# Order of the first mixer: value tiles beside the first modulation tiles, gates behind them, then queries and keys

## The reference

```python
def modulate(h, shift, scale):
    return h * (1.0 + scale[:, None, :]) + shift[:, None, :]

sh1, sc1, g1, sh2, sc2, g2 = jnp.split(jnp.einsum('bd,de->be', jax.nn.silu(c), ada_w) + ada_b, 6, axis=-1)
h = modulate(rmsnorm(x, norm_mix_g), sh1, sc1)
y = mlstm_mixer(h, ...)          # below
x = x + g1[:, None, :] * y

def mlstm_mixer(h, w_in, conv_w, b_if, hnorm_g, w_out):
    proj = jnp.einsum('bsd,de->bse', h, w_in)
    qk, v, o, gates = jnp.split(proj, ...)       # 1024, 1024, 1024 and 16 columns
    q, k = jnp.split(jax.nn.silu(causal_conv(qk, conv_w)), 2, axis=-1)
    ...                                          # per head: decays from the gates, scores q k, times v, over a denominator
    hh = rmsnorm(hh, hnorm_g) * jax.nn.sigmoid(o)
    return jnp.einsum('bse,ed->bsd', hh, w_out)
```

## Time and profile before

| | |
|---|---|
| median of 3 runs | 2536.34 us (2536.04 to 2536.48) |
| profiled execution, its span | 2535.0 us |
| PE busy in the span | 2494.9 us (98%) |
| DVE, ACT, POOL busy | 2040.5, 1492.4, 345.5 us |
| moved by DMA | 509 MB, 201 GB/s on average |

### The profile page before, as it was taken

How to read it: one execution, slowest core, us unless ns; L and a number is a source line. 1 busy time by engine, 2 the same in 40 slices (tenths; PEclk the granted TensorE clock), 3 DMA queues, 4 the chain that set the end, 5 groups by cost and what they waited for, 6 DMA issues and landing times.

```text
span 2535.0 us, 44017 instructions
## 1 busy us (share of the span) xinstructions
PE 2494.9 (98%) x14932; PEld 2170.5 (86%) x14932; DVE 2040.5 (80%) x3770; ACT 1492.4 (59%) x2489; POOL 345.5 (14%) x212
## 2 busy tenths in 40 slices
PE   7999999999999999999999999999999999999998
PEld 6789988888888888889988888888888888899887
DVE  7789979899888877679888998666667886688766
ACT  4455576666666656555677666665564555463553
POOL 4017600000000003527500000000000001000000
PEclk8999999999999999999999999999999999999999
DMA  7854576776888885435666776566555355553654
GB/s 270 284 167 165 195 238 191 201 208 204 302 292 288 284 258 162 142 122 170 210 217 193 206 199 209 183 200 202 194 191 190 127 188 184 193 177 107 199 183 141
DMA packets 142991, 509.07 MB, mean 201 GB/s; under 512 B 19200, under 2 KB 19256, under 8 KB 142560
## 3 DMA queue, kind: packets, MB, share of 16 engines
q1 hardware_dynamic: 135600, 481.90, 57.3%
q0 software_dynamic: 7216, 24.85, 5.1%
HBM read 488.84 MB, written 1.07 MB: 193 GB/s over the span
## 4 chain that ended last, share of the span: by engine, by line
PE 87%; DVE 5%; DMA 4%; ACT 2%; issue 1%; POOL 1%; SPq 0%; DVEq 0%; ACTq 0%
PE ps L243 51%; PE ps L249 19%; PE ps L250 9%; DMA weight_ring<-in_stream 4%; PE ps L1528 2%; ACT weight_split L269 1%; DVE weight_split L278 1%; POOL weight_split L278 1%; PE ps L2735 1%; PE ps L1492 1%; DVE arena L745 0%; DVE hT_split L503 0%; PE ps L457 0%; DVE stat L628 0%; DVE x L625 0%
## 5 line engine op out<-in xcount | busy, mean ns | idle before, releaser
L269 ACT ACTIVATE weight_split<-weight_ring 128x1024 fp32r<-128x1024 f32 x800 | 848.8, 1062 | 224.5 <-DMA weight_ring<-in_stream 132.9
L243 PE MATMUL ps<-weight_split,hidden_split 128*128 128x512 f32 x3948 | 911.8, 390 | 0.4 <-DVE hidden_split L1821 0.3
L278 DVE TENSOR_TENSOR weight_split<-weight_ring,weight_split 128x1024 fp32r<-128x1024 f32 x653 | 791.4, 1221 | 135.2 <-ACT weight_split L269 132.0
L243 PEld LDWEIGHTS ps<-weight_split,hidden_split 128*128 128x128 f32 x3948 | 736.0, 188 | 157.1 <-issue 1.0
L249 PE MATMUL ps<-hT_split,weight_split 128*128 128x512 f32 x2000 | 721.9, 402 | 0.5 <-DVE hT_split L503 0.4
L250 PE MATMUL ps<-hT_split,weight_split 128*128 128x256 f32 x2000 | 559.5, 280 | 0.0
L243 PE MATMUL ps<-hT_split,weight_split 128*128 128x256 f32 x3672 | 462.8, 285 | 3.0 <-DVE hT_split L503 0.8
L243 PEld LDWEIGHTS ps<-hT_split,weight_split 128*128 128x128 f32 x3672 | 447.3, 192 | 10.3 <-issue 5.9
L249 PEld LDWEIGHTS ps<-hT_split,weight_split 128*128 128x128 f32 x2000 | 375.7, 188 | 84.5 <-DVE hT_split L503 1.1
L250 PEld LDWEIGHTS ps<-hT_split,weight_split 128*128 128x128 f32 x2000 | 377.8, 189 | 2.6
L278 POOL TENSOR_TENSOR weight_split<-weight_ring,weight_split 128x1024 fp32r<-128x1024 f32 x115 | 279.1, 2433 | 115.5 <-ACT weight_split L269 85.2
(11 more groups left out here) (381 smaller groups left out, 2078.3 us busy)
## 6 DMA issues: line engine op xcount, KB each, us to landing
weight_ring<-in_stream SPq DMA_DIRECT2D x912, 512.0 KB, 4.2
weight_split<-weight_ring POOLq DMA_DIRECT2D x32, 512.0 KB, 5.3
arena<-gate_rows SPq DMA_DIRECT2D x3, 512.0 KB, 4.8
x<-in_x SPq DMA_DIRECT2D x1, 1024.0 KB, 5.1
arena<-mlstm_m_rows POOLq DMA_DIRECT2D x1, 1024.0 KB, 6.5
arena<-in_ln_mix_g POOLq DMA_DIRECT2D x2, 512.0 KB, 5.8
arena<-in_ln_mix_b POOLq DMA_DIRECT2D x2, 512.0 KB, 7.8
arena<-in_ln_ffn_g POOLq DMA_DIRECT2D x2, 512.0 KB, 4.7
```

The source lines that it names most:

```text
L243: mm = pe.matmul(out_, stationary(s_part), moving(m_part), start=start and n == 0, stop=stop and n == 2, skip_group_check=True)
L269: act.activation(wsplit[:, n % SPLITS, HIGH, :], ring[:, slot(POS[n]), :], ACT.Copy).then_inc(high_ready, 1)
L278: eng.tensor_tensor(w[:, REST, :], ring[:, slot(POS[n]), :], w[:, HIGH, :].bitcast(fp32), ALU.subtract).then_inc(split_ready, 1)
```

## The change

- The 16 first modulation tiles are reordered and all are dots now: scale chunk c, shift chunk c, for c = 0 to 7. After each pair DVE adds the bias and finishes the gain of that one chunk (`first_mods_dve`), so each chunk of the normed input can be made at once.
- Eight value tiles are the first tiles of TensorE. They and the modulation tiles 16 to 21 come through six further slots in `arena` (`side`), loaded by SP between the ring's loads. TensorE multiplies value tile c when chunk c is there, and the gates of chunk c-2 behind it. The 80 idle transposes are gone.
- Queries and keys follow, then the heads. The second half's modulation tiles (16 to 38) are all used in the head stage, three per head where there were two, and 39 in the output stage.
- The rests of value tiles 0 to 5, of all queries and keys and of all eight output-gate tiles are made by POOL; DVE makes those of value tiles 6 and 7 and of the output stage.
- silu of c is computed on a row that the DMA has spread over the partitions (512 KB written), in place of a spreading by TensorE.

The stream keeps its tiles and their number; their order and the part that comes by `side` are changed.

```diff
+V_TILES, SIDE, SIDE_ADA = 8, 6, range(16, 22)
-SEGMENTS = [("ada", "a", 16), ("mlstm", "s", 8), ("mlstm_v", "sa", 8), ("mlstm_o", "saa", 7), ("mlstm_o_end", "sa", 1),
-            ("mlstm_out", "s", 4), ("mlstm_out_ada", "sa", 1), ("mlstm_out_end", "s", 3),
+SEGMENTS = [("ada", "a", 16), ("mlstm", "s", 8), ("mlstm_o", "s", 4), ("mlstm_o_ada", "aaas", 4), ("mlstm_o_end", "a", 3),
+            ("mlstm_out", "s", 2), ("mlstm_out_ada", "a", 2), ("mlstm_out_mid", "s", 3), ("mlstm_last_ada", "a", 1), ("mlstm_out_end", "s", 3),
...
+        def first_dot_dve(a, products):
+            c, row = a // 2, 1 - a % 2
...
+            dve.tensor_tensor_reduce(products, ada_loaded(a), silu_row[:], 1.0, 0.0, ALU.mult, ALU.add, dots[:, row, c:c + 1]).then_inc(ada_used, 1)
...
         def mlstm_pool():
...
-            rests_pool(ML_T + 1, 3)
+            rests_pool(ML_V, 6)
+            rests_pool(ML_T, 4)
 
             pool.wait_ge(ml_gate_dve, M_READY)
             pool.dma_start(ml_rows.rearrange("(h t) -> h t", t=T), ml_M).then_inc(ml_M_moved, 16)
-            for n in range(ML_T + 4, ML_T + 6):
-                rest(pool, n)
+            rest(pool, ML_T + 4)
             pool.wait_ge(ml_M_moved, M_OUT)
             pool.dma_start(ml_Mb.rearrange("p h t -> p (h t)"), ml_rows.partition_broadcast(128)).then_inc(ml_M_moved, 16)
-            for n in range(ML_T + 6, ML_T + 10):
+            for n in range(ML_T + 5, ML_H + 8):
                 rest(pool, n)
...
+            def beside_v(c):
+                if c == 2:
+                    pe.wait_ge(ml_par, 16 * 7)
+                    pe.wait_ge(gate_w_ready, 1)
+                if c >= 2:
+                    gates(c - 2)
+            lin_rows(ML_V, 0, 0, between=beside_v)
+            gates(6)
+            gates(7).then_inc(ml_gates, 1)
...
         def mlstm_act():
...
+            high(ML_V)
+            modulated(0)
+            for c in range(1, 8):
+                modulated(c)
+                high(ML_V + c)
             highs_act(ML_T, 3)
...
         def mlstm_dve():
...
+            for c in range(8):
+                first_dot_dve(2 * c, ml_acc[:, 1])
...
+                first_dot_dve(2 * c + 1, ml_acc[:, 1])
+                first_mods_dve(c)
...
+                if c:
+                    chunk_split_dve(c - 1)
+            chunk_split_dve(7)
+            splits_until(dve, ML_V + 6)
+            rest(dve, ML_V + 6)
+            rest(dve, ML_V + 7)
...
-                    for a in (26 + 2 * h, 27 + 2 * h):
+                    for a in range(19 + 3 * h, 22 + 3 * h):
                         ada_dve(a, ml_acc[:, 1])
...
                 if h == 6:
-                    gated(6)
-                    ada_dve(38, ml_acc[:, 1])
+                    for a in (37, 38):
+                        ada_dve(a, ml_acc[:, 1])
+                    splits_until(dve, ML_O)
                     rest(dve, ML_O)
+                    rest(dve, ML_O + 1)
                     two_out(0)
-                else:
-                    rest(dve, ML_T + 18 + h)
-                    gated(h)
...
+            side_load(0)
+            side_load(1)
+            side_after = {1: (2,), 3: (3,), 5: (4,), 7: (5,), 9: (6,), 11: (7,), 15: (8, 9, 10, 11), 17: (12, 13)}
```

More of the change, by code:

```diff
@@ L73 @@
 GROUPS = len(CHUNK_GROUPS)
-OUT_GROUPS = [4 if n == 3 else GROUPS for n in range(9)]
+OUT_GROUPS = [{0: 8, 3: 4}.get(n, GROUPS) for n in range(9)]
 SRC_PARTS = {0: 3, 1: 5, 2: 5, 4: 5}
@@ L189, in build @@
         tile_full = [sem(f"tile_full{s}") for s in range(RING)]
+        side_full = [sem(f"side_tile_full{s}") for s in range(SIDE)]
         tiles_used = sem("tiles_used")
@@ L260, in splits_until, with loaded @@
             eng.wait_ge(split_ready, n)
+        def loaded(n):
+            return side[:, n % SIDE, :] if n < V_TILES else ring[:, slot(POS[n]), :]
         def high(n, i=0, step=1):
             d = stride(POS, n, step, 2) if not isinstance(i, int) else 0
-            act.wait_ge(tile_full[slot(POS[n])], i * (16 * d // RING) + full(POS[n]))
+            if n < V_TILES:
+                act.wait_ge(side_full[n % SIDE], 16 * (n // SIDE + 1))
+            else:
+                act.wait_ge(tile_full[slot(POS[n])], i * (16 * d // RING) + full(POS[n]))
             if n >= SPLITS:
                 act.wait_ge(tiles_used, i * step + (n - SPLITS + 1))
-            act.activation(wsplit[:, n % SPLITS, HIGH, :], ring[:, slot(POS[n]), :], ACT.Copy).then_inc(high_ready, 1)
+            act.activation(wsplit[:, n % SPLITS, HIGH, :], loaded(n), ACT.Copy).then_inc(high_ready, 1)
         def highs_act(n0, count):
@@ L277, in rest @@
             w = wsplit[:, n % SPLITS]
-            eng.tensor_tensor(w[:, REST, :], ring[:, slot(POS[n]), :], w[:, HIGH, :].bitcast(fp32), ALU.subtract).then_inc(split_ready, 1)
+            eng.tensor_tensor(w[:, REST, :], loaded(n), w[:, HIGH, :].bitcast(fp32), ALU.subtract).then_inc(split_ready, 1)
         def rests_pool(n0, count):
@@ L749, in ada_dve, with rows_summed @@
                 dve.tensor_tensor(mods[:, row, :], mods[:, row, :], dots[:, row % 2], ALU.add).then_inc(mod_ready, 1)
[L751 to L764, removed]
-            for c in range(8):
-                mm = pe.matmul(ps[:, bank + c // 4, (c % 4) * 128:(c % 4 + 1) * 128], silu_c[:, c:c + 1].broadcast_to([128, 128]), ident[:],
-                               start=True, stop=True)
-            mm.then_inc(silu_spread, 1)
-        def silu_row_act(bank):
-            act.wait_ge(silu_spread, 1)
-            act.activation(silu_row[:], ps[:, bank:bank + 2, :].rearrange("p a b -> p (a b)"), ACT.Copy).then_inc(silu_row_ready, 1)
+        def rows_summed(row):
+            return row - 1
         def scale_dve(norm):
             k, _, scale = NORMS[norm]
-            dve.wait_ge(mod_ready, scale + 1)
+            dve.wait_ge(mod_ready, rows_summed(scale))
             dve.scalar_tensor_tensor(out=gains[:, k, :], in0=mods[:, scale, :], scalar=1.0, in1=gains[:, k, :], op0=ALU.add,
@@ L808, in gate_spread_pe @@
             row = GATE_ROW[k]
-            pe.wait_ge(mod_ready, row + 1)
+            pe.wait_ge(mod_ready, rows_summed(row))
             for c in range(8):
@@ L1239, in mlstm_act @@
                 if h < 5:
-                    high(ML_T + 19 + h)
+                    high(ML_H + 3 + h)
                 if h == 4:
@@ L3111, in _ @@
                 hi = min(hi, len(KINDS) - RING)
-                times = (hi - lo) // period
+                times = (hi - lo) // period if lo > max(side_after) else 0
                 s_step, a_step = (pattern.count(kind) * period // len(pattern) for kind in "sa")
@@ L3283, in lay_out @@
     stream = np.empty((len(KINDS), 128, D), split.dtype)
-    stream[POS], stream[ADA_POS] = split, mod_rows
+    stream[POS[V_TILES:]] = split[V_TILES:]
+    ada_streamed = [n for n in range(len(ADA_POS)) if n not in SIDE_ADA]
+    stream[[ADA_POS[n] for n in ada_streamed]] = mod_rows[ada_streamed]
     def columns(rows):
@@ L3290, in lay_out @@
         "stream": stream,
+        "side": np.concatenate([split[:V_TILES], mod_rows[SIDE_ADA[0]:SIDE_ADA[-1] + 1]], 0),
         "mods": columns([*bias0, *bias1[:2], *a["kv_ada_b"].reshape(2, D), *bias1[2:]]),
```

211 lines of the change are left out of this document (102 added, 109 removed).

## The result

| | before | changed |
|---|---|---|
| median us (lowest to highest) | 2536.41 (2536.04 to 2538.31), 4 runs | 2546.20 (2541.51 to 2548.84), 4 runs |
| ratio | | 1.0037, 95% interval 1.0025 to 1.0049 |
| span of the profiled execution | 2535.0 | 2539.5 |
| start of the output stage in it | 143.03 | 148.56 |

The account below looks back on a forecast made before the run. TensorE, busy 98%, was taken as the bound, with slack only in the first 36 us. The output stage moves from 143.0 to 156.7, so 2536.3 + 13.7 = 2550.0 us; eight-in-ten range 2532 to 2558.

Parts of the forecast that it names:

- The row that decides: Trace rows behind the gates: DVE operations with both SBUF inputs wait out POOL's rest, so each rest costs dots 2.41 us.
- Rival 1: Dots run unhindered beside POOL's rests; 2534 us, or 2529 without late loads, against 2536.3 before; chance 0.25.
- late loads: Head stage: ring loads for the dots land late, charged about 1 us, up to 5.
- the spreads: Before the output stage: two more spreads and the last squares on TensorE, 1.6 us.
- Its size: Cost to DVE of one POOL rest beside a dot, taken as 2.41 us; six in the start, 14.5 us.
- Part 1: Start to end of gates: DVE's last split at 57.1, gates end at 66.2 against 39.9, 26.3 us later.
- DVE's own work: DVE's time without POOL's rests: 33.7 us up to the last input split, 44.9 from the first weighing on.
- Rival 3: TensorE's clock stays low at the end of the chunks; 7 us on top of the forecast, 2557; chance 0.08.
- Part 2: Gates' end to first head: 27.0 us against 54.1 before, first head at 93.2, 0.8 us earlier.
- Part 3: First head to output stage: DVE becomes the bound; output stage at 156.7 against 143.0, 13.7 us later.
- the slot's turn of 8.7 us: Head stage: the "s" slot's load, high part, rest and issue, about equal to DVE's 7.5 us per head.

Follow-up runs that it names:

- e2: Changed kernel with POOL's 22 rests each replaced by two fills that read nothing, low parts left out of the computation; 2530.53 us, 0.9980 of before.
- e4: Changed kernel with 14 idle TensorE transposes behind the gates in each of chunks 2 to 5; 2543.77 us, 1.0030 of before.
- e3: Changed kernel with dots 22 to 36 reading tiles already in the side slots, their 15 loads left out; 2539.36 us, 1.0011 of before.
- e9: e7 with dot rows 22 to 33 loaded through the six side slots, nothing left out; 2532.18 us, 0.9981 of before.
- e7: Changed kernel with rests of value tiles 0 to 5 on DVE and dots 16 to 18 made earlier; 2536.00 us, 1.0001 of before.
- e0: The changed kernel again, unaltered, for a second profile; 2544.84 us, 1.0036 of before.
- e10: e9 with the five head-stage rests of output-gate tiles (heads 3 to 7) on DVE too; 2530.35 us, 0.9972 of before.

## Why the prediction was right, point by point

It said 0.5% slower, and 0.4% was measured; 2550.0 against 2546.2 us. The output stage was put at 156.7 and came at 148.6, so the steps were right in kind and too large in size: 13.7 us later were predicted there, 5.5 measured. That the two times lie so close is in part luck, since the medians lie 4 us further apart than the two profiles.

- **The row that decides** held: a dot beside a rest of POOL stands still until it ends. e2 shows that POOL's writes and its being busy don't do this, which leaves its reading. Rival 1 (dots unhindered) is what e2 looks like: it is 5.6 us faster than the kernel before, where that rival had 2 to 7. (Its 141 for the output stage with late loads lacks the 1.6 of the spreads that its 135.8 has, and by its own terms its first head is at 82.9 and the weighing at 88.3.)
- **Its size** was off. 2.41 us was charged for each of six rests, 14.5; the five stretched dots cost 9.9 together (15.98 - 5 x 1.22) and the addition 2.1, in all 12.0. The rest starts 0.26 us before the dot that it stops (27.76 and 28.02), and that dot ends 1.07 behind the rest where it takes 1.22 alone, so 1.98 is lost and not 2.41.
- **Part 1** put DVE's last split at 57.1; it ended at 53.3. The first dot was at 9.98, not 8.9. DVE's own work was 31.3 (53.3 - 9.98 - 12.0) and not 33.7: per chunk, two dots took 2.64 (48.88 to 51.52) where 2.76 were charged, and bias and gain 0.27 (51.52 to 51.79) where 0.45 were, as the last chunk shows, which has no rest of POOL beside it. The two own rests, the two late tiles and the gates took 8.4 us more, where 9.1 were given. Rival 3 did not occur: the clock (the third number from the end) was at half, 1.2 GHz, in stretches up to about 47 us, but was back for the last tiles, and e4 shows that the low stretches did not matter. The last chunk on DVE, and the clock:

```profile
48.88 1.22 DVE L756 CUSTOM_DVE_ANT_0 arena<-weight_ring,silu_c_row 128x1024 f32<-128x1024 f32 x1
...
50.25 1.23 DVE L756 CUSTOM_DVE_ANT_0 arena<-weight_ring,silu_c_row 128x1024 f32<-128x1024 f32 x1
...
51.52 0.17 DVE L761 TENSOR_TENSOR mods<-mods,stat 128x2 f32<-128x2 f32 x1
...
51.79 0.29 DVE L1274 CAST hT_split<-arena 128x256 fp32r<-128x256 f32 x1
```

```profile
44.00:46.00 2.00, 2.00 (x6) 1.55 (x6) 1.86 (x3) 0.37 (x1) 1.55 (x1) 0.50 1.00 401
46.00:60.00 14.00, 11.17 (x49) 8.61 (x49) 9.18 (x18) 5.98 (x7) 5.14 (x3) 0.95 0.84 315
```

- **Part 2** took 25.7 (61.77 to 87.43) for 27.0.
- **Part 3** took 61.1 (87.43 to 148.56) for 63.5. The first weighing ended 6.2 behind the first head (5.4 predicted), with TensorE waiting 3.2 for 2.3. Behind it, three terms were wrong. The rests were charged 10.6 and cost 6.3 (the five dots took 12.35). Late loads were charged 1.0, with "up to 5" beside it, and DVE waited 6.5 for them. DVE's own work was charged 44.9 and took 40.5: from the weighing's end at 93.63 to 146.93, where TensorE goes on, are 53.3, less 6.3 and 6.5. One operation of DVE starts a little before the record of the one ahead ends (a weighing of 0.55 at 102.13, the gating of 0.41 at 102.60, the next dot at 102.93), and the sum took the full lengths. e3 and e9 show that late loads are a real term (5.5 us in e3, and 4.9 at the output stage from e7 to e9).
- **What hides behind what.** The prediction took the slot's turn of 8.7 us as about equal to DVE's 7.5 per head, and charged 1 us. The turns were 9.5, 7.2 and 7.7 us (ACT's high parts of the tiles in that slot start at 104.86, 114.38, 121.53 and 129.24), and the heads followed: 9.4, 6.8 and 7.4 us from one first dot to the next (107.72, 117.11, 123.86, 131.23), with DVE waiting for a load at each of the last three.
- **From the trace to the medians.** From the output stage to the end the profiles of before, changed and e0 to e10 have 2390.9 to 2396.2 us of the same work. The changed kernel's profile is the lowest of these, which is a part of why the medians show 4 us more than it does. e0's profile shows one place where such time lies, the low clock behind TensorE's last wait (9.98 us for the 36 matmuls in place of 8.39; 9.99 in e2). It is 1.6 us of the 4; how often it falls there in the timed runs and where the others lie isn't shown, and stays open.

## What to carry to other kernels

Before work is given to GpSimd because VectorE is full, look for VectorE operations with both inputs in SBUF beside it: if GpSimd reads, they stop for the rest of its operation, and the same work on VectorE can be cheaper (1.14 against 1.98 us here). In a queue of loads over few slots, ask of each load what must be finished before its slot is free; what is needed early must not stand behind the slot that turns slowest, and a helper's work put between the two may close a loop. Here the head rests on VectorE cost 5 us with the loop closed and brought 1.8 once it was cut.

## What the runs showed of the hardware

- GpSimd's fills of 128 x 1024 (0.95 us each) did not stretch a dot of VectorE that ran beside them (1.23 us), its subtractions of the same size did (up to 3.22). The Trainium skill (SBUF — State Buffer, section Who interferes with whom) says the same: a VectorE instruction with two SBUF inputs contends with a GpSimd instruction that reads SBUF, not with one that only writes it. e2's rows agree. A cast of VectorE (one input, 128 x 256) beside a fill did wait: in e2 it took 0.67 us at 18.34 in place of 0.29, and ended 0.14 behind the fill.
- The exclusion works both ways: the rest of POOL at 105.98 took 3.19 us in place of the usual 2.4, with a dot in progress when it began (105.69 to 106.92).
- With DVE waiting for loads in most chunks (e2), 401 GB/s were moved from 8 to 36 us, where the kernel before had 339 at a DMA share of 0.96: a share near one was not the end of what the queues could bring.
- That TensorE multiplies both parts of a split tile exactly, as the description of the kernel has it, no run here tests. Nothing in the argument rests on it.
